# Two-layer attention trunk on one core: memory keys from raw rows, first weights split a stage earlier, later sums in the latent heads

## What is computed

```python
def _memory_heads(q_flat, mem, ln_g, w_kv, g_qn, g_kn):
    q = _rms(q_flat.reshape(b, s, N_MEM_HEADS, MEM_HEAD_DIM), g_qn)
    kv = (_rms(mem, ln_g) @ w_kv).reshape(b, mem.shape[1], N_MEM_HEADS, 2 * MEM_HEAD_DIM)
    k = _rms(kv[..., :MEM_HEAD_DIM], g_kn)
    v = kv[..., MEM_HEAD_DIM:]
    sc = jnp.einsum('bqhd,bkhd->bhqk', q, k).astype(jnp.float32) * (MEM_HEAD_DIM ** -0.5)
    p = jax.nn.softmax(sc, axis=-1)
    o = jnp.einsum('bhqk,bkhd->bqhd', p.astype(v.dtype), v)
```

## Time and profile before

| what | value |
|---|---|
| median of 3 runs | 2671.93 us (2670.9 to 2675.89) |
| profiled execution, its own time | 2675.89 us |
| span of the profile | 2674.2 us |
| PE busy | 2532.8 us (95%) |
| DVE, ACT, POOL busy | 1729.3, 1312.1, 1119.3 us |
| memory phase, layer 0 | 0 to 80.25 us |
| memory attention, layer 0 | 80.25 to 153 us |
| memory phase, layer 1 | 1310 to 1372.25 us |
| memory attention, layer 1 | 1372.25 to 1446.7 us |
| latent heads | 1524 to 1933 us |

### The profile page before, as it was taken

How to read it: one execution, slowest core, us unless ns; L and a number is a source line. 1 busy time by engine, 2 the same in 40 slices (tenths; PEclk the granted TensorE clock), 3 DMA queues, 4 the chain that set the end, 5 groups by cost and what they waited for, 6 DMA issues and landing times. The chain is left out here.

```text
span 2674.2 us, 37095 instructions
## 1 busy us (share of the span) xinstructions
PE 2532.8 (95%) x12000; PEld 2051.9 (77%) x12000; DVE 1729.3 (65%) x2659; ACT 1312.1 (49%) x2487; POOL 1119.3 (42%) x845
## 2 busy tenths in 40 slices
PE   6899999989999999999888989999799999999999
PEld 5777777667788888888676877777687888888887
DVE  5567778855865655478654277777748665665595
ACT  6467777744433333444554356666535333333443
POOL 2134445311465566555310432223003765665554
PEclk9899999999999999999989999999899999999999
DMA  3211110143222232674211100000152322323843
GB/s 127 55 32 32 32 33 9 32 173 111 79 98 102 96 112 87 228 236 147 83 38 37 34 16 22 23 21 21 49 183 98 115 98 91 109 102 131 291 129 118
DMA packets 182859, 242.74 MB, mean 91 GB/s; under 512 B 31440, under 2 KB 105936, under 8 KB 182736
## 3 DMA queue, kind: packets, MB, share of 16 engines
q1 hardware_dynamic: 182736, 241.19, 27.3%
HBM read 175.60 MB, written 65.54 MB: 90 GB/s over the span
## 5 line engine op out<-in xcount | busy, mean ns | idle before, releaser
L2255 POOL TENSOR_TENSOR l0s_run_lo<-l0s_run,l0s_run_hi 128x512 fp32r<-128x512 f32 (+2 forms) x120 | 143.5, 1196 | 216.4 <-DVE l0s_run_hi L2408 216.4
L471 POOL TENSOR_TENSOR l1f_wd_lo<-l1f_d,l1f_wd_hi 128x512 fp32r<-128x512 f32 x77 | 108.2, 1406 | 106.1 <-ACT l1f_wd_hi L546 106.0
L471 POOL TENSOR_TENSOR l0f_wd_lo<-l0f_d,l0f_wd_hi 128x512 fp32r<-128x512 f32 x77 | 110.5, 1439 | 97.4 <-ACT l0f_wd_hi L546 97.3
L84 PE MATMUL banks<-l1f_T_hi,l1f_op_hi 128*128 128x512 f32 x352 | 137.4, 390 | 0.9 <-DVE l1f_T_lo L691 0.9
L84 PE MATMUL banks<-l0f_T_hi,l0f_op_hi 128*128 128x512 f32 x352 | 137.4, 390 | 0.9 <-DVE l0f_T_lo L691 0.9
L86 PE MATMUL banks<-l0f_T_hi,l0f_op_lo 128*128 128x512 f32 x352 | 137.8, 392 | 0.0
L86 PE MATMUL banks<-l1f_T_hi,l1f_op_lo 128*128 128x512 f32 x352 | 137.8, 391 | 0.0
L85 PE MATMUL banks<-l1f_T_lo,l1f_op_hi 128*128 128x512 f32 x352 | 137.4, 390 | 0.0
L85 PE MATMUL banks<-l0f_T_lo,l0f_op_hi 128*128 128x512 f32 x352 | 137.4, 390 | 0.0
L433 POOL TENSOR_TENSOR l1f_s<-l1f_raw 128x512 f32<-128x512 f32 x44 | 66.4, 1510 | 153.5 <-DMA l1f_raw<-in_w_ffn_gu_dram 130.7
L503 ACT ACTIVATE l1f_op_hi<-l1f_s 128x512 fp32r<-128x512 f32 x88 | 55.2, 631 | 142.8 <-PE banks L86 141.0
(11 more groups left out here) (532 smaller groups left out, 8406.9 us busy)
## 6 DMA issues: line engine op xcount, KB each, us to landing
l0f_raw<-in_w_ffn_gu_dram SPq DMA_DIRECT2D x22, 1024.0 KB, 5.2
l1f_raw<-in_w_ffn_gu_dram SPq DMA_DIRECT2D x22, 1024.0 KB, 5.1
l0f_a_raw<-hidden_rows SPq DMA_DIRECT2D x77, 256.0 KB, 4.0
...
```

Source lines behind the costliest of these rows:

```text
L84: pe.matmul(out, l_hi, r_hi, start=first, stop=False, skip_group_check=True)
L471: pool.tensor_tensor(wd_lo[g % RING][:], held[HELD_AT[DOWN[p][1]]][i][:], as_f32(wd_hi[g % RING][:]), ALU.subtract).then_inc(wd_lo_done, 1)
L2255: pool.tensor_tensor(run_lo[x % NR][:, f:HALF], run[x % NR][:, f:HALF], as_f32(run_hi[x % NR][:, f:HALF]), ALU.subtract).then_inc(run_spli ...
```

## The change

In the memory phase of layer 0, PE transposes the raw rows of mem, the row factor `mrstd` goes into DVE's copy of keys and values out of the banks, and the key and value product stands ahead of the transposes of x. The loads, ACT and DVE are put in the matching order, two of the four weight splits go from POOL to DVE, and unit 1 no longer stands between the second half's transposes; unit 2 does. In both layers a new helper, `FirstWeights`, loads and splits the first weights of `FirstPair` (q and k) or `LatentKeys` (all) in the memory phase, so that `Ahead` keeps only v, or two query blocks, and `pe_at` begins at place 0. Tiles are moved to make room: two `q_sq` tiles of layer 1 lie where x lay, so ACT waits there until x is stored and normalised. In the latent heads `rq 0`, `kturn 0`, `rq 1` and `qnorm 1` stand one step later.

```diff
         def _(sp):
             if not early:
                 for t in range(NM):
                     sp.dma_start(mem_x[:, t, :], mem_dram[t * P:(t + 1) * P, :]).then_inc(m_in[t], 16)
+                with nc.allow_non_contiguous_dma("gain"):
+                    sp.dma_start(m.mcol[:], gain_columns(ln_mem)).then_inc(mcol_in, 16)
+                for n in range(4):
+                    sp.dma_start(m.raw[n][:], kv_rows[:, 2 * n:2 * n + 2, :]).then_inc(w_in[n], 16)
                 for t in range(4):
                     sp.dma_start(x[:, t, :], x_dram[t * P:(t + 1) * P, :]).then_inc(x_in[t], 16)
...
+            first.load(sp, normed[1])
...
                 constants.on_pool(pool)
-                for n in range(4):
+                for n in (0, 2):
...
+            first.lower(pool)
...
+                act.wait_ge(mcol_in, 16)
+                upper_memory()
                 for n in range(4):
                     act.wait_ge(w_in[n], 16)
                     act.activation(m.wkv_hi[n][:], m.raw[n][:], ACT.Copy).then_inc(w_hi_done, 1)
...
+                squares(0)
+                for n in range(4):
+                    act.wait_ge(wkv_lo_done[n], 1)
+                upper_query_weights()
+                squares_of_memory()
+                act.wait_ge(col_in, 16)
+                upper_normed(0)
+                squares(1)
+                act.wait_ge(g_in, 48)
+                queries(0)
+                deviations_of_keys()
+                upper_normed(1)
+                upper_keys_and_values()
+                queries(1)
             stack((0, 2))
+            first.upper(act, 0)
             queries(2)
             deviations_of_queries(0)
+            first.upper(act, 1)
             queries(3)
...
+                        last = dve.tensor_scalar(dst, src, m.mrstd[:, t:t + 1], None, ALU.mult)
...
+            else:
+                keys_and_values()
+                for c in range(ND):
+                    turn(0, c)
+                for c in range(ND):
+                    project(0, c)
+                for c in range(ND):
+                    project(1, c)
+                sums_of_queries(0)
+                for c in range(ND + 2):
+                    if c < ND:
+                        turn(1, c)
+                    if c >= 2:
+                        project(2, c - 2)
+                sums_of_queries(1)
+                turn_keys()
...
+class FirstWeights:
...
+    def load(self, sp, normed):
+
+        sp.wait_ge(normed, 4)
+        for raw, source, loaded in zip(self.raw, self.sources, self.loaded):
+            sp.dma_start(raw, source).then_inc(loaded, 16)
...
-        self.pe_at = {3 + i: (i // 2, i % 2) for i in range(12)}
-        self.dve_at = {4: [0], 6: [1], 7: ["h0"], 8: [2], 9: ["h1"], 10: [3], 11: ["h2"], 12: [4], 13: ["h3"], 14: [5]}
+        self.pe_at = {0: (0, 1), 1: (2,), 3: (3,), 5: (4,), 6: (5,), 7: (6,), 9: (7,), 11: (8,), 12: (9,), 13: (10,), 15: (11,)}
+        self.dve_at = {0: [0], 4: [1], 5: ["h0"], 6: [2], 8: ["h1"], 9: ["h2"], 10: [3], 11: ["h3"], 12: [4], 15: [5]}
...
-        self.pe_at = {3: 0, 5: 1, 7: 2, 9: 3, 11: 4, 13: 5, 14: 6, 15: 7}
-        self.dve_at = {4: (0,), 6: (1,), 8: (2,), 10: (3,), 12: (4,), 14: (5,), 15: (6, 7)}
+        self.pe_at = {0: 0, 1: 1, 3: 2, 5: 3, 7: 4, 9: 5, 11: 6, 13: 7}
+        self.dve_at = {0: (0,), 1: (1,), 4: (2,), 6: (3,), 8: (4,), 10: (5,), 12: (6,), 14: (7,)}
...
-              6: ["kv 3", "knorm 0", "wk"], 7: ["q 1 0", "ksum 1", "q 1 1", "q 1 2", "knorm 1"], 8: ["ss 0", "rq 0"],
...
+              6: ["kv 3", "knorm 0", "wk"], 7: ["q 1 0", "ksum 1", "q 1 1", "q 1 2", "knorm 1"], 8: ["ss 0"],
+              9: ["rq 0"], 10: ["kturn 0"], 11: ["kturn 1"], 12: ["qnorm 0", "q 2 0", "wq 0"], 13: ["q 2 1", "v0"], 15: ["q 2 2"],
+              16: ["q 3 0"], 17: ["q 3 1", "q 3 2"], 18: ["wq 1", "kturn 2"], 19: ["ss 1"],
+              20: ["rq 1", "qnorm 1"], 21: ["kturn 3"]}
```

269 lines of the change are left out of this document (161 added, 108 removed), and 3 rows, old and new, of the table extras.

## The result

The changed kernel takes 2641.8 us (median of 4 runs, 2635.08 to 2643.69) against 2673.91 (2670.9 to 2678.71) for the kernel before on the same chip: a ratio of 0.987, 95% interval 0.9854 to 0.9886. The forecast was 2634 with a range of 2625 to 2646. The profiled executions lie 32.2 us apart (spans 2674.2 and 2642.0), where I had summed 37.8. Single executions of the changed kernel lie up to 8.6 us apart.

A forecast was written before the change was run, and what follows sets the result against it. PE was taken as the bound, busy 95% of the span, so only its waits or slow stretches could give. Terms 12.2 + 8.9 + 14.7 + 2.0 = 37.8 us off 2675.9 gave 2638.1, less 4.0 for the runs' median 2634; range 2625 to 2646.

The forecast's parts named there:

- (a): Whole kernel: the gains come as summed, 2634 us, own range 2627 to 2641; chance 0.6.
- all four terms: Gains: layer 0's memory phase 12.2 us, memory attention 8.9 in layer 0 and 14.7 in layer 1, latent heads 2.0.
- the first query product at 31.5: Layer 0's memory phase: query products start at 31.5 and not at 40.65, 9.2 us earlier.
- 6.5 + 4 + 1.1 + 2.7: Layer 0's memory phase: `mcol` landing, eight mem chunks, ACT's weight copy, POOL's split; key and value product starts at 14.3.
- the 28 at which I called the prediction wrong: Layer 0's memory phase: the prediction is wrong if x's normalised rows come after 28.
- the old wait: Layer 0's memory phase: PE's 3.03 us wait at 52.67 should go, as unit 1 stands ahead of the second half's transposes.
- (c): Layer 0's memory phase: x too late or query products start at 1.2 GHz; 5 to 6 us less, 2640; chance 0.12.
- (d): Memory attentions: start stays bound by softmax chain or clock; 9 us less, 2643 to 2648; chance 0.1.
- The slow start: Layer 0's memory attention: the clock's slow start costs 0.5 us.
- The chain: Layer 0's memory attention: `half_out` to first `lower`, 6.3 us, exceeds 5.45 of PE work in five one-part jobs; costs 4.2.
- The base of 54.6: Layer 0's memory attention: PE work of eight jobs at 2.7 us and twelve parts at 2.75, 54.6 us.
- The first wait of 1.1: Layer 1's memory attention: first softmax rows ready after 6.5 us, scores and a unit cover 5.4; PE waits 1.1.

The follow-up runs named there:

- e_query_weight_late: Changed kernel, but POOL starts the lower part of the query weights only when DVE has normalised the first half of x; 2640.6 us.
- e_filled_end: Changed kernel with six more matmuls on PE at the end of each memory phase; 2634.7 us.
- e_dve_moved: Changed kernel with three of DVE's steps in layer 0's memory attention in other places; 2639.5 us.
- e_heads_only: Kernel before with nothing but the new table of the latent heads; 2671.5 us against 2675.2, ratio 0.9987.

## Why the prediction was right, step by step

The time of 2641.8 lies in the range of 2625 to 2646, but outside the own range of (a), 2627 to 2641: all four terms were too high, and the range held because it took in part of the rivals.

*Memory phase, layer 0: mis-sized, 7.5 for 12.2.* The step that failed is the first query product at 31.5; it came at 35.83. (The sum's own parts, 25.3 and 6.0 and 0.5, make 31.8.) Of these 4.3 us, 1.8 are the start of the product (16.12 for 14.3): ACT's table load of 1.28 was not in "6.5 + 4 + 1.1 + 2.7". Another 2.0 are the product's own pace, 13.0 us for 11.0, nine matmuls at half pace behind a wait of 4.04. Then comes x: I took 25.3 and it was 30.1, later even than the 28 at which I called the prediction wrong. Of these 4.8 us, some 2.6 are ACT: x landed at 17.42, near the 17.5 that I took, but DVE began at 23.00 and not 3 us after the landing, since the four squares came only behind four copies of weights (16.28). The other 2.3 are the multiplications, 7.10 where I took 4.8. My argument against that rival, "that POOL has only two pieces left", forgot a third, the query weights, and e_query_weight_late shows that this one made 7.10 of 2.74. All of x's lateness cost only 0.9 while the product was late too, and `turn(0)` then took 5.67 and not 6.5. Two late chains that end together cost like one, and that is luck. The later part went as foreseen: 36.9 us from the first query product to the attention and not 39.6, 2.7 for the 3.0 of the old wait.

*The rivals.* (c) gave 2640 and the time is 2641.8: of its two forms, x came too late, as it says, but the query products did not start at 1.2 GHz (0.23 a matmul from 36.14 on). Against (d) I had said that the low clock has no cause once PE is filled. That argument failed: PE was busy for all of the first 4 us and had 0.50 and 0.60, the values that I had named as a sign of being wrong (over the first 20 us it had 0.86 and 0.91).

*Memory attention, layer 0: 6.7 for 8.9.* By the table of terms the gain is 4.1 of waits and 3.4 of the clock, less 0.9 of the rest. Two terms of the sum were off against each other. The slow start, charged with 0.5, costs 2.6 in this kernel (e_filled_end). The chain, charged with 4.2 in five jobs, shows waits of 0.17, 1.48 and 1.20, and part of these was DVE's queue (e_dve_moved). The base of 54.6 was too low: in e_filled_end `values(7)` came 59.45 after the start, and without its waits that leaves 55.2, where my 54.6 - 0.9 is 53.7.

*Memory attention, layer 1: 12.7 for 14.7* (13.4 up to `values(7)`). The gain is 9.5 of waits and 2.9 of the clock; against the same old code in e_heads_only it would have been 15.6, so the size is known to some 3 us only. The first wait of 1.1 did not show, since scores and unit ran at 0.60 and covered it; with the full clock it was there with 1.17, and the phase was no shorter. Slow clock and chain take the same time there.

*Latent heads: right in its mechanism, too small in its size.* The waits for the copied sums are gone, and `kturn` waits 0.6 for `l1a_kt_lo`, the 0.5 named. But a place gives 0.44 and not 0.2. In the profile 2.3 of the 4.4 were lost at the opening and 0.5 behind the last place, so that the 1.5 near the forecast 2.0 is luck.

*Not in the sum:* 3.7 us in stages whose code hardly changed. 2.9 of them lie in the ffn, and nearly all of that in one place. Behind a wait of 3.00 for `l0f_op_lo`, 12 matmuls and 8 transposes took 6.47 us in the kernel before and 3.62 in the changed one, where the wait was the same 3.01:

```profile
667.61:674.08 6.47, 6.47 (x20) 5.25 (x21) 5.16 (x6) 2.42 (x4) 1.07 (x1) 0.53 0.00 0
653.03:656.65 3.62, 3.62 (x20) 3.10 (x21) 3.62 (x5) 1.86 (x3) 1.09 (x1) 1.00 0.00 0
```

In three of the fourteen profiles this place ran at half clock, in eleven at full, all with a wait of 3.0. What decides it stays open. The touched stages gave 28.4 of the 37.8 us, and the total came closer than its parts deserve.
